# Up projection: a weight sum by accumulating DMAs on GpSimd's queue, and the value stage's decay block at another place on VectorE

## The reference, cut to what matters

```python
proj = h @ w_in                        # bg, cg, ua, q, k, v, r, lr, ga, gb
log_a = log_sigmoid(lr @ w_a2 + b_a) / 16      # decays of the recurrence, per token
...                                    # gated conv, chunked recurrence, w_out, residual
a, gt = split(h2 @ w_up)               # 1024 -> 2 x 2816
f = (gelu(dwconv3_causal(a)) * gt) @ w_down
```

## Time and profile before

| what | us |
|---|---|
| median of 3 runs | 992.66 |
| lowest, highest | 992.54, 993.23 |
| profiled execution: time | 992.22 |
| profiled execution: span | 990.5 |
| TensorE busy | 972.6 (98% of the span) |
| VectorE, ScalarE, GpSimd busy | 588.2, 396.6, 198.9 |
| TensorE clock granted | full in all 40 slices |

### The profile page before, as it was taken

The page is one execution under the profiler, slowest core; times in us unless marked ns, Lnnn a source line. Parts: engine busy times, 40 slices in busy tenths (PEclk is TensorE's granted clock), DMA queues, the critical chain, the costliest instruction groups (busy, mean ns, idle before and its releaser), DMA issues.

```text
span 990.5 us, 18686 instructions
## 1 busy us (share of the span) xinstructions
PE 972.6 (98%) x7695; PEld 885.2 (89%) x7695; DVE 588.2 (59%) x919; ACT 396.6 (40%) x601; POOL 198.9 (20%) x113
## 2 busy tenths in 40 slices
PE   5999999999999999999999999999999999999997
PEld 4889789999999999999988799999999999888886
DVE  3535936666467554534546788777777778760204
ACT  4556443423443342543554444333333333533212
POOL 2040042233334333332352000000000000013430
PEclk9999999999999999999999999999999999999999
DMA  9772175695564677336345033232332331322212
GB/s 320 235 139 107 41 187 147 116 134 109 160 182 130 122 200 76 108 90 166 107 148 166 20 109 86 64 86 86 86 85 86 91 97 52 125 85 85 86 51 96
DMA packets 145029, 115.60 MB, mean 117 GB/s; under 512 B 11225, under 2 KB 121585, under 8 KB 144945
## 3 DMA queue, kind: packets, MB, share of 16 engines
q1 hardware_dynamic: 144849, 114.38, 43.9%
q10 hardware_dynamic: 96, 0.04, 0.0%
HBM read 107.02 MB, written 7.35 MB: 115 GB/s over the span
## 4 chain that ended last, share of the span: by engine, by line
PE 94%; DVE 2%; SPq 1%; ACT 1%; DMA 1%; issue 1%; DVEq 0%
PE pair L2105 51%; PE pair L2211 12%; PE pair L2582 10%; PE pair L2535 5%; PE pair L2228 2%; PE pair L2095 2%; PE pair L2346 1%; PE pair L2319 1%; DMA raw<-in_w_in 1%; PE pair L2411 1%; PE pair L2400 1%; PE pair L2455 1%; PE pair L2203 1%; PE pair L2415 1%; PE pair L2204 1%
## 5 line engine op out<-in xcount | busy, mean ns | idle before, releaser
L2105 PE MATMUL pair<-h_hi,w_hi 128*128 128x288 f32 x1264 | 282.2, 301 | 0.1
L2105 PE MATMUL pair<-h_hi,w_lo 128*128 128x288 f32 x1264 | 275.7, 296 | 0.0
L2105 PE MATMUL pair<-h_lo,w_hi 128*128 128x288 f32 x1264 | 275.5, 295 | 0.0
L932 POOL TENSOR_TENSOR w_lo<-raw,w_hi 128x1024 fp32r<-128x1024 f32 x45 | 108.5, 2414 | 582.1 <-ACT w_hi L1007 523.1
L2105 PEld LDWEIGHTS pair<-h_hi,w_hi 128*128 128x128 f32 x1264 | 204.6, 188 | 18.4 <-issue 16.7
L2105 PEld LDWEIGHTS pair<-h_lo,w_hi 128*128 128x128 f32 x1264 | 205.0, 188 | 0.0
L2105 PEld LDWEIGHTS pair<-h_hi,w_lo 128*128 128x128 f32 x1264 | 205.1, 188 | 0.0
L1007 ACT ACTIVATE w_hi<-raw 128x1024 fp32r<-128x1024 f32 x58 | 61.1, 1057 | 143.7 <-PE pair L2205 71.5
L932 POOL TENSOR_TENSOR w_lo<-raw_c,w_hi 128x1024 fp32r<-128x1024 f32 x24 | 67.5, 2818 | 114.3 <-ACT w_hi L1007 114.3
L2211 PE MATMUL pair<-w_hi,f_hi 128*128 128x512 f32 x176 | 68.8, 391 | 0.0
L2211 PE MATMUL pair<-w_lo,f_hi 128*128 128x512 f32 x176 | 68.7, 390 | 0.0
(11 more groups left out here) (372 smaller groups left out, 1657.0 us busy)
## 6 DMA issues: line engine op xcount, KB each, us to landing
raw_c<-in_w_ada SPq DMA_DIRECT2D x32, 512.0 KB, 5.1
raw<-in_w_in SPq DMA_DIRECT2D x224, 64.0 KB, 3.6
raw_c<-in_w_in SPq DMA_DIRECT2D x192, 64.0 KB, 3.6
raw<-in_w_up SPq DMA_DIRECT2D x24, 512.0 KB, 4.8
raw<-in_w_down SPq DMA_DIRECT2D x22, 512.0 KB, 3.8
raw_up<-in_w_up SPq DMA_DIRECT2D x20, 512.0 KB, 3.8
ada_first<-in_w_ada SPq DMA_DIRECT2D x16, 512.0 KB, 9.8
s_in<-in_state_gla SPq DMA_DIRECT2D x16, 256.0 KB, 3.6
```

Of the source, the lines that this page charges most:

```text
L932: pool.tensor_tensor(lo, raw_tile(n)[:, :], hi.bitcast(F32), ALU.subtract).then_inc(S("w_lo_done"), 1)
L2105: ins = pe.matmul(bank[pair][:, half, 0:HALF], w[:, i, :], x[:, i, HALF * half:HALF * half + HALF], start=i == 0 and p == 0, stop=i == KT ...
```

## The change

Two things are done.

In the value stage, DVE's decay block leaves its place ahead of tile 4: the subtraction stands behind the low part of tile 7, the two memsets behind that of tile 8. The sums of T4 leave their place behind T2's (at tile 5) and stand behind the low part of tile 10, so that T3 is made ahead of T4; SP's wait for the last T4 sum becomes a wait for twelve sums instead of ten.

In the up stage, for each of the nine odd couples, w_sum1 = a21 + a22 is made by two DMAs that GpSimd issues: one that copies a21 into w_sum1, and behind its end one that adds a22 to it. They wait for the load of a21 and a22, and for the low part of factor 4 of the odd couple before (the last reader of w_sum1). DVE's first addition goes, and `factors` waits for the second DMA's end (`s_first`). ACT's factor 3 waits for it too. The counts of `s_add` fall from four to three for a couple.

The semaphores `p_sel` and `lr_zero` are merged into `p_set`, with the counts shifted.

```diff
-        return {T1: 4, T2: 6, T4: 8, T3: 10}[kind]
+        return {T1: 4, T2: 6, T3: 8, T4: 10}[kind]
...
-            sp.wait_ge(S("lr_zero"), 2)
+            sp.wait_ge(S("p_set"), 17)
...
-                    sp.wait_ge(S("s_add"), 5 + 4 * sevens(j))
+                    sp.wait_ge(S("s_add"), 5 + 3 * sevens(j))
...
+            for j in range(5, FT, 2):
+                name, count = up_landed[j, 1]
+                pool.wait_ge(S(name), count)
+                pool.wait_ge(S("w_lo_done"), TILE_UP + (op_at(j - 2) + 5 if j > 5 else 0))
+                for i in range(2):
+                    pool.dma_start(w_sum1[:, :], up_raw(j, 1)[:, 512 * i:512 * i + 512],
+                                   accum_op=ALU.add if i else ALU.bypass).then_inc(S("s_first"), 16)
+                    pool.wait_ge(S("s_first"), 32 * sevens(j) + 16 * i + 16)
...
+                elif q == 3:
+                    act.wait_ge(S("s_first"), 32 * (sevens(j) + 1))
                 else:
-                    act.wait_ge(S("s_add"), 5 + 4 * sevens(j) + {2: 2, 3: 1, 4: 4, 5: 3}[q])
+                    act.wait_ge(S("s_add"), 5 + 3 * sevens(j) + {2: 1, 4: 3, 5: 2}[q])
...
             for m in range(16):
-                if m == 4:
-                    dve.wait_ge(S("z_abs"), 6)
-                    dve.wait_ge(S("z_min"), 4)
-                    dve.tensor_tensor(pre[:, :, :], pre[:, :, :], suf[:, :, :], ALU.subtract).then_inc(S("z_min"), 1)
-                    dve.wait_ge(S("z_min"), 5)
-                    dve.memset(suf[:, :, :], 0.0).then_inc(S("level_set"), 1)
-                    dve.memset(ext[:, 0:2], 0.0).then_inc(S("zeroed"), 1)
...
                 elif m == 5:
                     v_sum(T2, B22, T1)
-                    v_sum(T4, B21, T2)
+                elif m == 7:
+                    dve.wait_ge(S("z_abs"), 6)
+                    dve.wait_ge(S("z_min"), 4)
+                    dve.tensor_tensor(pre[:, :, :], pre[:, :, :], suf[:, :, :], ALU.subtract).then_inc(S("z_min"), 1)
+                elif m == 8:
+                    dve.wait_ge(S("z_min"), 5)
+                    dve.memset(suf[:, :, :], 0.0).then_inc(S("level_set"), 1)
+                    dve.memset(ext[:, 0:2], 0.0).then_inc(S("zeroed"), 1)
                 elif m == 9:
                     v_sum(T3, B22, B12)
+                elif m == 10:
+                    v_sum(T4, B21, T2)
...
             def factors(j):
-                at_ = 5 + 4 * sevens(j)
-                for x in range(2):
-                    name, count = up_landed[j, x]
-                    dve.wait_ge(S(name), count)
-                (a11, _), (a21, a22) = ((up_raw(j, x)[:, 0:512], up_raw(j, x)[:, 512:1024]) for x in range(2))
-                dve.tensor_tensor(w_sum1[:, :], a21, a22, ALU.add).then_inc(S("s_add"), 1)
-                dve.wait_ge(S("s_add"), at_ + 1)
+                name, count = up_landed[j, 0]
+                dve.wait_ge(S(name), count)
+                dve.wait_ge(S("s_first"), 32 * (sevens(j) + 1))
+                (a11, _), (a21, _) = ((up_raw(j, x)[:, 0:512], up_raw(j, x)[:, 512:1024]) for x in range(2))
                 dve.tensor_tensor(w_sum2[:, :], w_sum1[:, :], a11, ALU.subtract).then_inc(S("s_add"), 1)
                 dve.tensor_tensor(a21, a11, a21, ALU.subtract).then_inc(S("s_add"), 1)
```

More of the change, by code:

```diff
@@ L913, in _ @@
                 pool.affine_select(out=m, in_=m, compare_op=ALU.is_ge, fill=0.0, base=0,
-                                   pattern=[[-2 * B, 64 // B], [0, B]], channel_multiplier=1).then_inc(S("p_sel"), 1)
-                pool.wait_ge(S("p_sel"), i + 1)
+                                   pattern=[[-2 * B, 64 // B], [0, B]], channel_multiplier=1).then_inc(S("p_set"), 1)
+                pool.wait_ge(S("p_set"), 5 + i + 1)
                 pool.affine_select(out=m, in_=m, compare_op=ALU.is_ge, fill=0.0, base=B - 1,
@@ L919, in _ @@
             pool.affine_select(out=sides, in_=sides, compare_op=ALU.is_ge, fill=0.0, base=0,
-                               pattern=[[-72, 2], [-32, 2], [-2 * TS, 2]], channel_multiplier=1).then_inc(S("p_sel"), 1)
-            pool.wait_ge(S("p_sel"), 8)
+                               pattern=[[-72, 2], [-32, 2], [-2 * TS, 2]], channel_multiplier=1).then_inc(S("p_set"), 1)
+            pool.wait_ge(S("p_set"), 13)
             pool.affine_select(out=sides, in_=sides, compare_op=ALU.is_ge, fill=0.0, base=TS - 1,
[L923 to L926, removed]
+                               pattern=[[72, 2], [32, 2], [2 * TS, 2]], channel_multiplier=-1).then_inc(S("p_set"), 1)
+            pool.wait_ge(S("p_set"), 14)
+            pool.tensor_tensor(own[:, 4:6, :], own[:, 0:2, :], own[:, 2:4, :], ALU.add).then_inc(S("p_set"), 1)
+            pool.wait_ge(S("p_set"), 15)
             pool.tensor_tensor(own[:, 6, :], own[:, 4, :], own[:, 5, :], ALU.add).then_inc(S("consts"), 1)
@@ L937, in low_of_pair @@
                     .then_inc(S("w_lo_done"), 1)
-            pool.memset(w_lr[:, :, RANK:32], 0.0).then_inc(S("lr_zero"), 1)
-            pool.memset(w_a2[:, :], 0.0).then_inc(S("lr_zero"), 1)
+            pool.memset(w_lr[:, :, RANK:32], 0.0).then_inc(S("p_set"), 1)
+            pool.memset(w_a2[:, :], 0.0).then_inc(S("p_set"), 1)
             pool.wait_ge(S("w_lo_done"), 3)
@@ L953, in _ @@
             pool.memset(q_own[:, :], 0.0).then_inc(S("p_set"), 1)
-            pool.wait_ge(S("p_set"), 6)
+            pool.wait_ge(S("p_set"), 18)
             pool.wait_ge(S("back"), KT)
@@ L1806, in last_factor @@
             def last_factor(j):
-                dve.wait_ge(S("s_add"), 5 + 4 * sevens(j) + 3)
+                dve.wait_ge(S("s_add"), 5 + 3 * sevens(j) + 2)
                 dve.wait_ge(S("w_lo_done"), TILE_UP + op_at(j) + 4)
@@ L2171, in _ @@
             pe.wait_ge(S("lr_in"), 16)
-            pe.wait_ge(S("lr_zero"), 2)
+            pe.wait_ge(S("p_set"), 17)
             pe.wait_ge(S("prm_done"), 1)
```

## The result

The change makes the kernel slower: 999.61 us against 992.60 us for the kernel before on the same chip, a ratio of 1.0075 with a 95% interval of 1.0063 to 1.0086. The profiled execution spans 997.4 us where the one before spans 990.5. I had forecast 990.7 us, and had given slower a chance of 0.23. The measured time lies inside my range; the sign is wrong.

A forecast was written before the change was run, and what follows sets the result against it. The prediction took TensorE to bound the kernel. The value stage would gain 1.98 us and the up stage lose nothing: 992.66 - 1.98 = 990.7 us, range 990.0 to 1004.1.

The forecast's parts named there:

- What bounds the kernel: Whole kernel: TensorE, busy 972.6 of 990.5 us, so a change wins only what TensorE waits for.
- The value stage: Both TensorE waits, ahead of tiles 4 and 6, go: 1.98 us gained, up to 0.15 more.
- Rival 2: Gain eaten by low parts of tiles 8 to 11, late C1 loads or a slight edge overrun: 0.5 to 2 us; chance 0.14.
- rival 3: Value stage: ACT, not VectorE, holds tile 6, so only 0.54 us is gained, 992.1; chance 0.03.
- The up stage, mechanism: Odd couples: VectorE's wait for the DMA pair is hidden up to an edge; beyond it TensorE loses time with each load.
- The loop: Up stage, load to load: beyond the edge it exceeds TensorE's 23.94 us, and VectorE falls back with each of eight loads.
- the edge in C: Up stage: up to 7.6 us factor 6's low part is on time and TensorE sees nothing.
- C: Up stage: time from the landing of a21 and a22 to the second DMA's end; taken as 7.2 us.
- TensorE's wait for factor 4's low part: Up stage, sign of a wrong forecast: grows from couple to couple up to a steady C - 7.6.
- the 6 us of cover for factor 0: Up stage: factor 0's low part, ready near 730, is wanted by TensorE at 736.46, over 6 us later.
- the value taken for C: Up stage: 7.2 us for two 256 KB DMAs in a row, 0.4 us from the edge, no loss.
- the upper bound: Up stage: 9.6 us for the DMA pair, said to count contention twice; 13.4 us lost, 1004.1.

The follow-up runs named there:

- e3: The change, but GpSimd makes the weight sum with one addition of its own instead of two DMAs; 990.09 us, ratio 0.9976 to the kernel before.
- e1: The value stage's part alone, with the up stage of the kernel before; 990.19 us against 992.68, ratio 0.9976.
- e4: The change, but SP issues the even couple's loads behind the end of the DMA pair; 990.40 us, ratio 0.9979 to the kernel before.
- e6: The change with GpSimd's own addition instead of the DMAs, and ten time-filling memsets ahead of it; 990.42 us, ratio 0.9979 to the kernel before.
- e8: Only the decay block's move in the value stage, up stage of the kernel before; 990.04 us, ratio 0.9978.
- e9: The kernel before with only T4's sums moved behind tile 10 and SP's wait for twelve sums; 991.08 us, ratio 0.9987.
- e7: The change with GpSimd's own addition instead of the DMAs, and sixteen time-filling memsets ahead of it; 1012.99 us, ratio 1.0206 to the kernel before.

## Why the prediction was right and wrong

*What bounds the kernel: right.* Only TensorE's waits counted. Taking nine sums off VectorE gained nothing (e3 against e1).

*The value stage: right, a little small.* I had 1.98 us plus up to 0.15; the stage is 2.21 us shorter, and the times of e1, e3, e4, e6 and e8 lie 1.8 to 2.6 below the kernel before on their chips. VectorE's order came out within 1 us of the one worked out: low part 6 ended at 105.6 (106.1 worked out), T4's sums at 121.4 (122.4). Rival 2, the gain eaten by late C1 loads, did not happen (e1). Nor did rival 3, that ScalarE holds tile 6: moving T4's sums alone took its wait away (e9).

*The up stage, mechanism: right.* The loop, the edge in C, and TensorE's wait for factor 4's low part are what the trace shows. Two sizes in it were off. The edge is 8.09 us, not 7.6: between factors 4 and 6 I counted two idle gaps of the earlier trace rows, 0.47 us, and VectorE made up 0.92 there, since a third gap of 0.17 falls away and since a row that waits for nothing starts some 0.08 before the one ahead of it ends. In full, factor 6's low part ends 742.67 - 727.19 = 15.48 us behind w_sum2 in the kernel before and 746.64 - 734.61 = 12.03 in the kernel after, which is 3.45 us of cover where I had 2.95. And the 6 us of cover for factor 0 did not last: once VectorE falls back from load to load, TensorE waits there too, in couple 11 for example:

```profile
712.06 0.40 PE L2591 MATMUL pair<-h_hi,w_hi 128*128 128x288 f32 x1 [0.45 <-DVE w_lo L1805]
```

So the wait for factor 4's low part, 0.8 us at most, is only a part of what C is over the edge, where I had written that it would be all of it.

*The step that failed: the value taken for C*, 7.2 us, two times the row of a 256 KB load. It is 9.39. The second DMA was right (3.48 against 3.6). The first took 5.44, because SP's loads for couple 14 had the engines. I had that row in hand, and put the contention into the upper bound with the remark that 9.6 counted it twice; it was there once, and as large as a whole DMA: 5.44 - 2.66 = 2.8 us (e4). The right reading would have been one DMA by a row without contention, plus one that must wait until most of SP's megabyte has been moved. From 0.4 us below an edge I should not have given the case beyond it 0.23.

Put together with the measured terms: 8 x (9.39 - 8.09) = 10.4, less about 2 of cover (I had 2.6), less 2.2 gained, is 6 us; 7.0 was measured. The rest is that couple 13 doesn't stand for all eight. Couple 7's copy took 6.33 us, which used up the cover at once: TensorE lost 0.35 us in that couple already (11.50 from its first matmul to the next couple's, where it was 11.15). From there VectorE's w_sum2 of couples 7 and 21 show the seven steps that are left:

```profile
658.20 0.69 DVE L1812 TENSOR_TENSOR w_sum<-w_sum,raw_up 128x512 f32<-128x512 f32 x1 [6.26 <-DMA w_sum<-raw_up]
...
834.97 0.69 DVE L1812 TENSOR_TENSOR w_sum<-w_sum,raw_up 128x512 f32<-128x512 f32 x1 [4.65 <-DMA w_sum<-raw_up]
```

These are 176.77 us, 9.19 over seven times 23.94. With the 0.35 that is 9.54, what the up stage grew by.

The estimate from the Trainium skill ("DMA: Bandwidth & Descriptors", Anatomy of one DMA — SWDGE (gpsimd) path), 2.6 us for 256 KB, fits the lone copy (2.66) and not the adding DMA (3.43). The same page of the Trainium skill (Issuing engines are not separate DMA queues) says that DMAs of all queues interleave on the same 16 engines. The trace agrees that GpSimd's copy and SP's loads share the engines, and that decided this case: 5.44 us beside the loads and 2.66 without them (e4). It shows little interleaving before 728, when 0.01 of the copy's 0.26 MB had moved.

## What to carry to other kernels

Here a step moved from an engine to two DMAs traded 0.69 us of that engine's busy time for 9.39 us of latency. Where the step lies in a loop of load, work and next load, add up that loop before and after: in these runs nothing showed as long as it was shorter than TensorE's period (e4, e6), and what lay beyond was paid once for every turn (the change, e7). Price such a DMA beside what the queues carry in that very microsecond, and look for a load that can stand behind it: here one wait on SyncE gave back all 9 us.

## What the runs showed of the hardware

Two loads of 512 KB issued 1 to 3 us ahead made a copy of 256 KB within SBUF take 5.44 instead of 2.66 us. An accumulating DMA of 256 KB took 3.48 us where a plain one at its place took 2.35. GpSimd's own addition of the same 128 x 512 tile took 1.29 us, less than either. And TensorE's loss by two short waits was 2.21 us where its waits were given as 1.7: they count from the modelled end of a matmul, and the starts behind them come slower for a while (0.30 us from the first to the second matmul of tile 6, where 0.23 is usual).
